# Small score units last in pass one, the sparse logarithm inside pass two, and a cache load in two halves, in a hybrid decoder step

## What is computed

```
# prompt: gating (group A), forgetting attention (B), sparse attention (C)
y_a = u * (w_s @ v + b_s)                       # v normalized per row and head
s = q @ k.T * SCALE + cq - ck                   # B; causal; p = softmax(s); y_b = p @ v
k_cmp, v_cmp = nsa_compress(kc), nsa_compress(vc)
y_c = g0*o_cmp + g1*o_sel + g2*o_win            # C; g = sigmoid gates
# sample: the same with kv_past = fox_kv_c[page_table], rows_past = nsa_kv_c[page_table]
kv_all = concatenate([kv_past, kv_new]);  y_b = fox_attend(q, ..., kv_all[:, :, 0], kv_all[:, :, 1], ...)
x = LN(alpha*x + mixed @ w_out);  x = LN(alpha*x + moe(x))
```

## Time and profile before

| | |
|---|---|
| time, median of 3 runs (lowest, highest) | 1206.99 us (1206.28, 1207.24) |
| profiled execution, its own time | 1205.49 us |
| its span | 1203.7 us |
| busy: PE, DVE, ACT, POOL | 93%, 41%, 34%, 11% |
| mean granted clock of PE | 0.948 of 2.4 GHz |
| single pieces of the trace: the convolution of one 512-column chunk on DVE; the short projection of tile 8; the compression of the prompt (unit 12) on PE | 2.8 us; 3.6 us; 7.3 us |
| SP's wait for the second compression, before the first forgetting pages | 14.5 us |
| from `so_ready` 1 to SP's first page load of the last job | 2.9 us |
| share of the chain that ended last: PE, DMA, DVE, issue, ACT, SP's queue | 67%, 10%, 8%, 7%, 3%, 3% |

### The profile page before, as it was taken

One profiled execution on the slowest core, in us unless ns is written; L12 is line 12 of the kernel. 1 busy time (PEld: TensorE's weight loads), 2 busy tenths in 40 slices (PEclk: granted clock), 3 DMA queues, 4 the chain that ended last, 5 costly groups with the idle time before them and its releaser, 6 DMA issues.

```text
span 1203.7 us, 14869 instructions
## 1 busy us (share of the span) xinstructions
PE 1120.8 (93%) x4726; PEld 603.4 (50%) x4727; DVE 491.4 (41%) x1009; ACT 412.1 (34%) x761; POOL 134.0 (11%) x201
## 2 busy tenths in 40 slices
PE   8999999999999979999999799999489999999991
PEld 7646755444545534445555445555444444444440
DVE  2112334346543452342235323333703566565664
ACT  0101333447221145543433101111022655656563
POOL 4100000000000010000000000000002334343432
PEclk9999999999998879999999799998579999999996
DMA  8312332532110031116433525112375679888822
GB/s 238 102 36 102 110 141 70 181 129 53 70 70 1 1 65 54 30 53 19 127 84 95 188 98 182 55 51 79 114 261 195 212 251 387 295 297 267 305 101 79
DMA packets 117995, 157.92 MB, mean 131 GB/s; under 512 B 30362, under 2 KB 89050, under 8 KB 117914
## 3 DMA queue, kind: packets, MB, share of 16 engines
q1 hardware_dynamic: 90474, 103.98, 28.3%
q10 hardware_dynamic: 16416, 30.17, 6.9%
q0 software_dynamic: 11056, 23.10, 5.6%
HBM read 139.47 MB, written 52.73 MB: 160 GB/s over the span
## 4 chain that ended last, share of the span: by engine, by line
PE 67%; DMA 10%; DVE 8%; issue 7%; ACT 3%; SPq 3%; POOL 1%; ACTq 1%; DVEq 0%; POOLq 0%
PE psum_all L1441 19%; PE psum_all L1950 10%; PE psum_all L1557 8%; DMA arena<-slot_rows,partner_now 5%; PE psum_all L1512 4%; PE psum_all L1588 3%; PE psum_all L1622 3%; PE psum_all L2036 2%; PE psum_all L1646 2%; DMA arena<-x_scratch,tok_now 2%; DVE arena L2733 1%; PE psum_all L1910 1%; DVE arena L2737 1%; PE psum_all L1614 1%; PE psum_all L1585 1%
## 5 line engine op out<-in xcount | busy, mean ns | idle before, releaser
L1441 PE MATMUL psum_all<-arena 128*128 128x512 f32 (+7 forms) x800 | 233.5, 463 | 0.2 <-DMA arena<-in_w_in 0.2
L2036 PE MATMUL psum_all<-arena 128*128 x400 | 180.0, 604 | 2.9 <-issue 1.9
L1441 PEld LDWEIGHTS psum_all<-arena 128*128 128x128 f32 (+1 forms) x800 | 130.1, 181 | 90.2 <-issue 63.2
L2036 PEld LDWEIGHTS psum_all<-arena 128*128 128x128 f32 x400 | 75.4, 194 | 90.4 <-issue 90.4
L1950 PE MATMUL psum_all<-arena 128*128 128x512 f32 (+1 forms) x288 | 119.4, 597 | 0.0
L1111 ACT ACTIVATE psum_all<-psum_all,neg_max 128x128 f32<-128x128 f32 (+7 forms) x96 | 65.7, 684 | 141.2 <-DVE neg_max L2168 140.9
L1557 PE MATMUL psum_all<-arena 128*128 128x512 f32 (+1 forms) x288 | 103.3, 515 | 0.0
L2024 PE MATMUL psum_all<-arena 128*128 x200 | 90.3, 594 | 1.2 <-ACT arena L1386 1.2
L1950 PEld LDWEIGHTS psum_all<-arena 128*128 128x128 f32 (+1 forms) x288 | 50.8, 186 | 62.2 <-issue 62.1
L1557 PEld LDWEIGHTS psum_all<-arena 128*128 128x128 f32 x288 | 48.9, 199 | 51.0 <-issue 50.6
L2168 DVE TENSOR_REDUCE neg_max<-psum_all 128x1 f32<-128x128 f32 (+7 forms) x96 | 65.1, 719 | 1.7
(11 more groups left out here) (414 smaller groups left out, 1489.5 us busy)
## 6 DMA issues: line engine op xcount, KB each, us to landing
slot_rows<-slot_rows ACTq DMA_DIRECT2D x8, 2048.0 KB, 8.7
arena<-in_w_exp_gate SPq DMA_DIRECT2D x16, 1024.0 KB, 8.5
arena<-in_w_exp_up SPq DMA_DIRECT2D x16, 1024.0 KB, 11.4
arena<-in_w_exp_down SPq DMA_DIRECT2D x16, 1024.0 KB, 14.0
slot_rows<-arena ACTq DMA_DIRECT2D x24, 512.0 KB
arena<-in_x_prompt SPq DMA_DIRECT2D x16, 512.0 KB, 4.1
arena<-in_cache_fox_kv SPq DMA_DIRECT2D x32, 256.0 KB, 3.2
arena<-in_w_in SPq DMA_DIRECT2D x2, 2048.0 KB, 11.5
```

The source lines that it names most:

```text
L1441: ins = nc.tensor.matmul(row_bank(j)[p0:p0 + n, 0:cn], xT[:, k, tok0(t):tok0(t) + n], wv[:, k, c0:c0 + cn], start=(k == 0), stop=(k == KD ...
L2036: ins = nc.tensor.matmul(psum[0][:], xT_slot[:, k, :], arena[:, bass.ds(w_at + k * 2 * F, 2 * F)], start=(k == 0), stop=(k == KD - 1))
```

## The change

Five edits, all in the order of work.

1. The sparse units run over query tiles 1 to 7 and then 0, so the last four units of pass one are those of tile 0. `STATS_AFTER` stays.
2. In the steps of pass one DVE scales and gates before it takes maxima and centers.
3. `log_sums` of the sparse half moves from the end of pass one to behind unit 12 of pass two on ACT, `make_shifts` to unit 13 on DVE, `turn_shifts` and `split_shifts` from unit 2 to unit 14. The turn now waits for `y_done` 2, since bank 7 holds the output of group 1 until then.
4. Pass two starts as its banks come free: unit 0 at `z_used` 11, unit 1 at `z_used` 12 with the gating done; the wait for all sums moves behind the scores of unit 2.
5. SP loads the pages of job `fox 1` in two rounds of halves: the keys once the 8 key units of `fox 0` are turned, then, when they have landed and `so_ready` is 1, the values. The product with values waits for the second count.

```diff
-        stats += [("nsa", qt, h) for qt in range(NT) for h in range(H)]
+        stats += [("nsa", qt, h) for qt in list(range(1, NT)) + [0] for h in range(H)]
...
+        LOGS_AT = COMP_P_AT
...
+            fox_units = sum(u == 0 for u, _, _ in units)
+            sp.wait_ge(kt_turned, fox_units)
+            load_pages(cache_fox_kv[0, :, :, 0].rearrange("n p h d -> n p (h d)"), fox_cache[:, :, 0:GW],
+                       4 * NPG, 4 * NPG, fox_cache_in)
+            sp.wait_ge(fox_cache_in, 16 * 4 * NPG * 2)
             sp.wait_ge(so_ready, 1)
-            load_pages(fox_pages, fox_cache, 4 * NPG, 4 * NPG, fox_cache_in)
+            load_pages(cache_fox_kv[0, :, :, 1].rearrange("n p h d -> n p (h d)"), fox_cache[:, :, GW:2 * GW],
+                       4 * NPG, 4 * NPG, fox_cache_in)
...
-            log_sums(N_ST, H * NT, N_COL)
...
                 exp_work(u)
+                if u == LOGS_AT:
+                    log_sums(N_ST, H * NT, N_COL)
...
                 elif u == 0:
+                    pe.wait_ge(z_used, 11)
+                    pe.wait_ge(sh_rows, 16 * 6)
+                else:
                     pe.wait_ge(z_used, 12)
                     pe.wait_ge(zg_used, TILES)
-                    pe.wait_ge(sh_rows, 16 * 6)
-                if u == 2:
-                    pe.wait_ge(st_summed, 2 * N_ST)
...
-                if kt == 0 and g == 1:
+                if kt == 0 and g == 3:
                     pe.wait_ge(sh_parts, 6)
...
                 if u == 2:
+                    pe.wait_ge(st_summed, 2 * N_ST)
+                if u == LOGS_AT + 2:
+                    pe.wait_ge(y_done, 2)
                     turn_shifts(1, H * NT, N_COL)
...
+                if br == "fox" and g:
+                    pe.wait_ge(fox_cache_in, 16 * 4 * NPG * 3)
...
-            make_shifts(1, H * NT, N_COL)
...
-                if u == 2:
+                if u == LOGS_AT + 1:
+                    make_shifts(1, H * NT, N_COL)
+                if u == LOGS_AT + 2:
                     split_shifts(1, 2 * H * NT)
```

More of the change, by code:

```diff
@@ L2321, in _ @@
                     convolve(f, c)
-                for n in stats_of(N_ROWJ + i):
-                    row_max(n)
-                if N_ROWJ + i in CENTER_AFTER:
-                    center_v(CENTER_AFTER[N_ROWJ + i])
                 if N_ROWJ + i in SCALE_AFTER:
@@ L2330, in _ @@
                     gate_u(GATE_AFTER[N_ROWJ + i])
+                for n in stats_of(N_ROWJ + i):
+                    row_max(n)
+                if N_ROWJ + i in CENTER_AFTER:
+                    center_v(CENTER_AFTER[N_ROWJ + i])
             dve.wait_ge(z_used, 12)
-            make_shifts(1, H * NT, N_COL)
             def mask_work(u):
```

## The result

The changed kernel took 1217.59 us, the median of 4 runs (1217.11 to 1218.31), where the kernel before took 1206.63 us on the same chip (4 runs, 1205.88 to 1207.24): a ratio of 1.0095, 95% interval 1.0060 to 1.0129. It is 11.0 us slower (the interval of the ratio is 7 to 16 us); 16.5 were forecast. The profiled execution has a span of 1215.1 us against 1203.7.

A forecast was written before the change was run, and what follows sets the result against it. PE, busy 93% of the span, bounds the kernel through its waits and lowered clock. Pass one +1.6, earlier `z_used` 12 -1.65, clock +2.0, logarithm +0.5, pages +16.7, sample stage -2.7: 1205.49 + 16.5 = 1222.0, median 1223.5, range 1214 to 1231.

The forecast's parts named there:

- Gating ahead: Pass one, steps with gating matmuls: PE's three waits for DVE go or shrink, gaining 3.7, 5.0 and 5.4, together -14.1 us.
- The two new waits: Pass one, behind gating tiles 5 and 6: second large unit waits 3.24 us for sums, plus 3.0 slow clock each: +12.5.
- order: Pass one to step 16's projection: bigger units done earlier put it 3.25 us later, given back at once after it.
- Into pass two: Up to unit 5: PE waits some 10 us for compression weights; `z_used` 12 1.65 us earlier; slow clock +2.0.
- The logarithm: Pass two: the moved logarithm's shift operations, wait for `y_done` 2 and split cost some 0.5 us, bounds 0 and 2.5.
- The pages: Unit 28: SP's page loop starts late behind the shifts; PE waits 14.7 us, plus 2.0 of clock: +16.7.
- The rival of early pages: Unit 28: page loads faster than their issue absorb SP's late start; the 16.7 term goes, 1206.8 us; chance 0.08.
- The sample stage: Keys' wait of 3.23 us goes, two loops delay `wo`; up to 1 us given back: -2.7, bounds 0 and -5.2.

The follow-up runs named there:

- the gating kernel: Kernel before the change, with only scale and gate moved ahead of maxima and centering on DVE: 1190.88 us, ratio 0.9896.
- rounds of eight: Changed kernel with 8 pages instead of 4 in each round of SP's page loop for the compressed rows: 1220.28 us, ratio 1.0139.
- `wo` early: Changed kernel with router and output projection loaded between keys and values of job `fox 1`, instead of behind both: 1218.08 us, ratio 1.0100.
- combined with `wo` early: Changed kernel with old unit order, position rows early, page loop halved around the shifts' rows, router and `wo` between `fox 1` keys and values: 1184.67 us, ratio 0.9848.

## Why the prediction was right, and where its sizes were off

**Gating ahead: right.** Forecast 3.7, 5.0 and 5.4. In the gating kernel, by starts of the same instructions, the three places gave 3.96, 5.22 and 5.91; the wait left over was 0.95 there and 1.19 in the changed kernel, without slow clock, as forecast from the 0.98 of the earlier trace rows. Of the nine kernels with the wait of 1.19, though, two ran the projection behind it in 8.41 and 8.34 us instead of 7.13 (rounds of eight; `wo` early).

**The two new waits: right in place, a little too dear.** 3.29 us each, forecast 3.24. The slow clock behind them was (2.50 - 1.35) + (8.77 - 7.13) = 2.8 and (2.32 - 1.35) + (7.81 - 7.13) = 1.65, where 3.0 was taken for each: 11.0 instead of 12.5. That pass one ends at -0.33 and not at +1.6 is these 1.5 and 0.4 of gating and order.

**Into pass two: right.** `z_used` 12 came 1.67 us earlier than step 16 (SP's L785 at -3.58 against -1.91), forecast 1.65; from it to unit 5 were 20.37 us, forecast 20.3; PE stood 11.46 us, forecast 10; the slow clock took 2.1, forecast 2.0.

**The logarithm: right.** 0.2 us by the table (-1.39 to -1.19), forecast 0.5.

**The pages: right, 1.7 us too dear.** From the mask of unit 14 on, SP took the rows at 480.92, and from there to PE's turn are 47.2 us, forecast 47.4. The wait was 13.98, forecast 14.7, and the clock cost 0.94 net, forecast 2.0, by the loss between the first page turn and the next (1.5 by the longer rows, less 0.5 of two small waits that the kernel before has there). The rival of early pages needed a loop of 32 us and is refuted by the 47.2: reading the table sets the pace, as the kernel with rounds of eight showed, and the DMA engines were 18% busy from 488 to 530. The rule cited from the Trainium skill (DMA: Bandwidth & Descriptors, the two cost components) is a fit for DMAs that GpSimd issues; these are SP's. It gives, as an estimate, 2.15 us for a page of 64 KB, where the median is 1.8, and 11.6 us for the 4 MB of `wo`, where the earlier trace rows has 15.5; of the loop it says nothing.

**The sample stage: the step that failed.** Forecast -2.7 with 0 as its upper end, found +0.36 in the traces (+13.79 at its start, +14.15 at the first product of `mix_out(1)`, 712.47 against 726.62) and nothing in the medians. Four parts: the wait for keys went, -2.87. The turn of the keys kept its slow clock (1.97 us where the earlier trace rows has 1.94), and +0.88 behind it. The prediction, and its low end of -5.2, had put this slow clock down to the wait for keys. The stretches show that the clock had fallen before that wait, first in the kernel before, which waits from 668.21 to 671.44, then in the changed kernel, where the keys' turn at 682.36 waits for nothing (stretch, us, busy times of PE, PEld, DVE, ACT, POOL, PEclk, DMA share, GB/s):

```profile
661.00:665.39 4.39, 2.67 (x69) 2.01 (x71) 2.34 (x7) 1.21 (x4) 0.00 (x0) 1.00 0.61 168
665.39:668.21 2.82, 1.78 (x49) 0.97 (x37) 0.98 (x5) 0.36 (x2) 0.00 (x0) 0.50 0.80 259
```

```profile
675.00:678.07 3.07, 1.86 (x49) 1.33 (x47) 1.79 (x5) 0.83 (x2) 0.00 (x0) 1.00 0.34 82
678.07:682.36 4.29, 2.72 (x52) 1.87 (x52) 1.54 (x8) 0.67 (x4) 0.00 (x0) 0.50 0.25 75
```

Both kernels have the same small waits for ACT and DVE there, of 0.4 to 1.0 us. Third, the product with values ran near full clock, 1.93 us, -1.64; so it did in two experiments (rounds of eight; combined with `wo` early) and in the ten others it took 3.15 to 3.64, so that is chance. Last, +3.99 at `wo`: it landed when it was forecast (709.57; forecast 695.5 + 13.8 = 709.3), PE was there 0.7 us sooner than forecast, and behind the wait of 1.94 came 2.1 us more of slow clock than before (`mix_out(0)` took 16.99 us, before 14.89). That clock is the term left out: the sum had up to 1 us for the new wait and nothing for the clock behind it.

**The rest** of the difference is no term. Of 16.5 forecast 11.4 came: less by 1.6 us at the start of this execution, 1.5 at the pairs, 0.4 in gating and order, 0.3 at the logarithm and 1.7 at the pages, more by 3.1 at the sample stage, and less by 2.75 between 807 and the end, 1.8 of it in the router's matmuls. The first and the last of these, 4.4 of the 5.1 us, no edit explains, and single executions of one kernel differ by as much: 25 of the kernel before on one chip took 1196.98 to 1210.84 us. Whether the medians hold them too is not shown.

## What to carry to other kernels

Before moving an operation, list what stands behind its result on every queue, the DMA queue's loops first: the 33 us for which SP stood waiting for the shifts cost nothing on the engines that make them, and 15 us through a loop of loads that did not even need them. Before reordering units between buffers, check pair by pair whether the second still finds a free one. And an early start is worth only as much as the next wait lets through; the 12 us that the change had made at the front of pass two were there to be had by loading the small tables ahead of the semaphore that only the large weights need.

## What the runs showed of the hardware that I had not expected

**The slow clock behind a wait does not grow with the wait.** After waits of 13.06, 13.98 and 18.17 us at the same instruction the granted clock stayed at 0.50 for 8.0, 3.2 and 9.0 us; in the four other kernels with this wait, of 13.37, 13.47, 13.51 and 13.90 us, for 7.6, 7.6, 7.9 and 3.7. In stretches of the changed kernel, then of the kernel with the logarithm at unit 15 (columns as above):

```profile
528.08:531.72 3.64, 3.64 (x16) 1.78 (x17) 2.35 (x7) 0.00 (x0) 0.00 (x0) 0.56 0.10 30
531.72:535.00 3.28, 3.28 (x22) 1.59 (x22) 2.18 (x4) 0.63 (x1) 0.00 (x0) 1.00 0.16 47
```

```profile
532.54:536.50 3.96, 3.96 (x16) 1.78 (x16) 2.63 (x8) 0.00 (x0) 0.00 (x0) 0.50 0.13 36
536.50:541.70 5.20, 5.20 (x20) 2.14 (x18) 1.90 (x3) 1.34 (x2) 0.00 (x0) 0.51 0.18 51
541.70:545.00 3.30, 3.30 (x21) 1.91 (x19) 0.00 (x0) 1.97 (x5) 0.00 (x0) 1.00 0.14 40
```

From that turn to the next such turn the seven kernels took 0.9 to 3.5 us more than the kernel before, so a term for the clock needs a range of some 2 us on each side, whatever its wait.

**A clock that falls while PE is busy.** The 48 matmuls of the router for the last tiles, with 16 columns each and no wait, are the same in all kernels. They took 5.68 us in the changed kernel and 7.46 in the kernel before:

```profile
832.98 7.46 PE L1910 MATMUL psum_all<-w_r,arena 128*128 128x16 f32 x48
```

In the twelve experiments they took 5.79 to 7.48. The granted clock was 0.94 over the first of the two stretches and 0.71 over the second, and 0.50 in both right behind it: it falls somewhere inside the group. That is up to 1.8 us by which two traces differ with no cause in either kernel, about as much as a whole term of the sum.
